# Expert gather with three row groups for U and three for V, V rows six groups behind, and the query block ahead of a chunk's weights

## The reference, cut to what matters

```python
q = (xblk @ w_query).reshape(B, TOKEN_BLOCK, N_PEER_HEADS, 2, SUBKEY_DIM)
s = jnp.einsum('bthpd,hpnd->bthpn', q, sub_keys)
vals, idx = lax.top_k(s, PEER_TOPK)
...
top_s, pos = lax.top_k(cand, PEER_TOPK)
eidx = jnp.take_along_axis(cand_idx, pos, axis=-1)
g = jax.nn.softmax(top_s, axis=-1)
h = jnp.einsum('btd,bthkd->bthk', xblk, expert_u[eidx])
act = jax.nn.gelu(h, approximate=False) * g
return jnp.einsum('bthk,bthkd->btd', act, expert_v[eidx])
```

## Time and profile before

| | us |
|---|---|
| median of 3 runs | 3295.08 |
| lowest and highest | 3289.69, 3298.97 |
| span of the profiled execution | 3263.7 |
| median less that span | 31.4 |
| expert gather, layer 0, first indirect DMA to last | 240.7 to 1010 |
| the same, layer 1 | 1230 to 1997 |

### The profile page before, as it was taken

The page is one execution under the profiler, slowest core; times in us unless marked ns, Lnnn a source line. Parts: engine busy times, 40 slices in busy tenths (PEclk is TensorE's granted clock), DMA queues, the critical chain, the costliest instruction groups (busy, mean ns, idle before and its releaser), DMA issues.

```text
span 3263.7 us, 34887 instructions
## 1 busy us (share of the span) xinstructions
PE 2431.9 (75%) x12607; PEld 1727.6 (53%) x12607; DVE 2088.5 (64%) x4416; ACT 933.8 (29%) x1486; POOL 1043.1 (32%) x1060
## 2 busy tenths in 40 slices
PE   5996555544546997555545545999999999999998
PEld 4754422221103764422221102789879988997797
DVE  7878576666656958576666654655555555556654
ACT  3511011110112421011101112544554446445543
POOL 0105566666663105566566663100010001000000
PEclk9998777766667998677666766989999999999999
DMA  9858999999999839999999998345534542554353
GB/s 363 299 209 332 353 374 380 378 379 365 361 378 341 295 139 342 350 370 394 377 359 372 356 365 307 131 143 191 180 130 155 180 168 82 190 194 155 110 193 123
DMA packets 308642, 886.31 MB, mean 272 GB/s; under 512 B 22824, under 2 KB 32144, under 8 KB 308240
## 3 DMA queue, kind: packets, MB, share of 16 engines
q0 software_dynamic: 147456, 536.94, 42.9%
q1 hardware_dynamic: 161040, 347.51, 29.9%
HBM read 883.32 MB, written 1.05 MB: 271 GB/s over the span
## 4 chain that ended last, share of the span: by engine, by line
PE 46%; issue 31%; DVE 9%; another core or an unknown queue 6%; DMA 4%; SPq 2%; ACT 2%; POOL 1%; DVEq 0%; ACTq 0%; POOLq 0%
PE lin L837 7%; PE lin L838 7%; PE lin L839 7%; PE psT L839 2%; PE psT L838 2%; PE psS L838 2%; PE psS L839 2%; PE psT L837 2%; PE psS L837 2%; PE lin L1141 2%; PE psS L1097 2%; PE psS L887 2%; DMA ring<-in_w_in 2%; PE lin L1014 1%
## 5 line engine op out<-in xcount | busy, mean ns | idle before, releaser
L2454 DVE CUSTOM_DVE_ANT_0 proj<-proj,psT 128x1024 f32<-128x1024 f32 x512 | 606.1, 1218 | 211.1 <-DMA proj<-in_expert_u,eidx 120.5
L1928 DVE TENSOR_TENSOR weights_split<-ring,weights_split 128x1024 fp32r<-128x1024 f32 (+1 forms) x360 | 431.5, 1207 | 376.2 <-ACT weights_split L1712 373.6
L2787 POOL DMA_INDIRECT proj<-in_expert_u,eidx x512 | 481.5, 940 | 424.7 <-DVEq L2430 212.7
L1712 ACT ACTIVATE weights_split<-ring 128x1024 fp32r<-128x1024 f32 (+1 forms) x376 | 391.5, 1046 | 467.7 <-PE lin L839 291.6
L1141 PE MATMUL lin<-vbuf,rowb 128*32 128x512 f32 x1024 | 252.0, 879 | 266.8 <-issue 180.4
L2823 POOL TENSOR_TENSOR weights_split<-ring,weights_split 128x1024 fp32r<-128x1024 f32 x16 | 37.9, 2376 | 995.3 <-ACT weights_split L1712 995.3
L1141 PE MATMUL lin<-ring,rowb 128*32 128x512 f32 x896 | 208.8, 755 | 153.1 <-issue 107.1
L837 PE MATMUL lin<-weights_split,xT_high 128*128 128x512 f32 (+1 forms) x736 | 295.0, 401 | 19.6 <-issue 8.2
L839 PE MATMUL lin<-weights_split,xT_high 128*128 128x512 f32 (+1 forms) x736 | 288.1, 391 | 0.0
L2800 POOL DMA_INDIRECT ring<-in_expert_v,pT x224 | 211.0, 942 | 231.4 <-remote 86.8
L2800 POOL DMA_INDIRECT vbuf<-in_expert_v,pT x256 | 241.2, 942 | 115.5 <-issue 76.5
(11 more groups left out here) (336 smaller groups left out, 4943.9 us busy)
## 6 DMA issues: line engine op xcount, KB each, us to landing
ring<-in_mlp_w_up SPq DMA_DIRECT2D x32, 2048.0 KB, 8.1
ring<-in_mlp_w_down SPq DMA_DIRECT2D x32, 2048.0 KB, 7.9
ring<-in_w_in SPq DMA_DIRECT2D x14, 2048.0 KB, 14.1
ring<-in_w_query SPq DMA_DIRECT2D x14, 2048.0 KB
vbuf<-in_ada_w SPq DMA_DIRECT2D x12, 2048.0 KB, 12.9
ring<-in_diff_w_in SPq DMA_DIRECT2D x11, 2048.0 KB, 8.1
proj<-in_ada_w SPq DMA_DIRECT2D x24, 512.0 KB, 5.1
ring<-in_moba_w_in SPq DMA_DIRECT2D x6, 2048.0 KB, 8.0
```

The lines of the kernel that those rows point to most:

```text
L1712: act.activation(part(p, 0, kind, w), raw_piece(slot, p, kind, w), ACT.Copy).then_inc(hi_ready, 1)
L1928: dve.tensor_tensor(part(p, 1, kind, w), raw_piece(slot, p, kind, w), part(p, 0, kind, w).bitcast(F32), ALU.subtract).then_inc(lo_ready, 1)
L2454: dve.tensor_tensor_reduce(ubuf[:, n % GB, :], ubuf[:, n % GB, :], x_row, 1.0, 0.0, ALU.mult, ALU.add, hdot[:, cb, k:k + 1]).then_inc(h_re ...
L2787: pool.indirect_dma_start(out=ubuf[:, (16 * c + k) % GB, :], out_offset=None, in_=table["u"], in_offset=bass.IndirectOffsetOnAxis(ap=eidx[ ...
```

## The change

U gets a third group of buffers, in ring slot 3, which was a V set; V keeps three sets. `UQUAD` says which U group goes where: the first four alternate between the two old ones, then the three rotate. So U(i) waits, but for the first few, for the dots of U(i-3), and V(q) for the sum of V(q-3). The last V group goes to U buffers. V(q) is issued behind U(q+6) for chunks 5 to 12, behind U(q+2) in chunks 0 and 1, and with a lag of 3, 4 and 5 in chunks 2 to 4 and of 5, 4 and 3 in the last three (`LAGS`). `stationaries(c)` of chunks 3 to 13 moves behind dot 3 of chunk c+1 (`SPREAD_BEHIND`, `SPREAD_STEP`), ahead of the quarter of the search there. In asking chunks from 4 on, keys, both halves of the query and the scores all come ahead of `weights_by_pair(c)`. `indices_by_pair(c+2)` comes ahead of a chunk's sums instead of between them.

```diff
-VLAG = 2
+NVB = 3
+GROUPS = 4 * PH * NT
+UQUAD = [0, 1, 0, 1] + [(2, 0, 1)[i % 3] for i in range(GROUPS - 4)]
+UBEFORE = [max([j for j in range(i) if UQUAD[j] == UQUAD[i]], default=None) for i in range(GROUPS)]
+VBUF = [q % NVB for q in range(GROUPS - 1)] + [NVB]
...
+SPREAD_BEHIND = range(3, NCH - 2)
+SPREAD_STEP = 3
+LAGS = [2, 2, 3, 4, 5] + [6] * (NCH - 8) + [5, 4, 3]
...
                 for c in range(1, NCH):
+                    if c in ASKED and c > 2:
+                        query_keys(ASKED[c])
+                        for part in range(4):
+                            query_rows(ASKED[c], part)
+                        key_scores(ASKED[c])
                     weights_by_pair(c)
-                    if c in ASKED and c > 1:
-                        query_keys(ASKED[c])
                     expert_sum(c)
...
                 for c in range(3, NCH):
-                    dots(c)
-                    stationaries(c)
+                    after = {4 * step + 3: [lambda step=step: topk_part(c + 2, step)] for step in range(4)} if c + 2 < NCH else {}
+                    if c - 1 in SPREAD_BEHIND:
+                        after[SPREAD_STEP] = [lambda: stationaries(c - 1)] + after.get(SPREAD_STEP, [])
+                    dots(c, after)
+                    if c not in SPREAD_BEHIND:
+                        stationaries(c)
...
-                    if n >= GB:
-                        pool.wait_ge(h_ready, n - GB + 4)
+                    if UBEFORE[i] is not None:
+                        pool.wait_ge(h_ready, 4 * UBEFORE[i] + 4)
...
-                        if 4 * c + g >= VLAG:
-                            v_rows(4 * c + g - VLAG)
+                        while q < NSET * NCH and q + LAGS[q // NSET] <= 4 * c + g:
+                            v_rows(q)
+                            q += 1
```

## The result

The changed kernel takes **3575.31 us** (median of 5 runs, 3571.02 to 3591.33) where the kernel before took 3298.97 in the same rounds: ratio **1.084**, 95% interval 1.082 to 1.087. I had predicted 3371 and a range up to 3465. Slower was right, the size wasn't: 276 us are lost and not 76.

The account below looks back on a forecast made before the run. Taken as bound: nearly full DMA plus POOL's pauses before V rows. Span 3263.7 plus 75.6 us for asking chunks gave 3339.3, with 31.4 around it 3371 us predicted; range 3240 to 3465.

Parts of the forecast that it names:

- What bounds the kernel: U(16) to U(60): DMA needs 41.2 us a chunk, chunks take 46.5; the gap is POOL's pauses before V rows, 78 us.
- The chain without lateness: From issue of U(4c+4) to issue of U(4c+8), through PE's sum and DVE's dots: 37.3 us plain, 58.6 us asking.
- The block of 21.3 us: Query block of asking chunks, between the sum of V(4c-1) and the weights: transposes, two halves, ACT's copies, scores.
- the excess: Asking chunks 6, 8 and 10: 63 us instead of 50.4, so 12.6 us each, 75.6 us in two layers.
- both bounds: Upper times of a chunk with reports late in full: 54.2 us plain, 72 us asking.
- I keep what plain chunks take now: Plain chunks stay at 45.7 us; the old pauses go and return as pauses before U rows.
- rival 1: Reports are late in full: plain chunks up to 54.2, asking ones 72 us; 3544 us in full, chance 0.17.
- The rest: Moved indices, first four chunks (up to 10 us gain a layer) and the end (up to 9 us loss): set at zero.
- nearly hidden: Query block in chunk 4: chunk 3's rows have lag 4 and land before chunk 4's dots end, so it costs little.
- The quarter of the search: DVE's search part on the chain, behind the stationaries and before four dots: 3.5 us taken.
- The 31.4 us around the span: Time added to the forecast span of 3339.3 us to give 3370.7 us.
- Rivals 2 and 3: 2: removed pauses pay for the query block, 3293 us, chance 0.13; 3: DVE's wait is covered, 3223 us, chance 0.24.

Follow-up runs that it names:

- Pacing: Three memsets of 0.33 us on POOL ahead of each group of four row issues, against the changed kernel otherwise unaltered: 3416 us, 1.041 of the kernel before.

## Why the prediction failed

**What bounds the kernel.** Right for the chip of the earlier trace rows: the pauses before V rows went (78 us to 24), and new ones came before U rows, with dots as releaser, as written. The rule that I had set aside, a core's share of about 358 GB/s (the Trainium skill, DMA: Bandwidth & Descriptors, Specifications), isn't what binds: 408 GB/s over 476 us.

**The chain without lateness: right.** It gave 37.3 us for plain chunks, under POOL's 39.8: measured 39.8 on the prompt chip. That is less than the 41.2 us of DMA that I had called a bound from below; over several chunks it still holds (374 GB/s in this stretch), since the DMA catches up in the pauses of the asking chunks. The chain gave 58.6 for asking ones: measured 829.0 - 770.5 = 58.5, and 57.9; the third is 64.0, behind a chunk of 35.3. The block of 21.3 us took 820.71 - 801.24 = 19.5.

**Luck in the excess.** The 37.8 us a layer that I forecast from U(16) to U(60) look right on the prompt chip, 512.1 - 476.2 = 35.9, but by two errors that cancel: the three asking chunks cost 180.4 - 124.8 = 55.6 us more, since they took 41 to 42 and not 50.4 before, and the other eight took 19.7 less.

**The step that failed: how much of the lateness falls on the chain.** The prediction had both bounds, 54.2 and 72 us. It kept 45.7 for plain chunks ("I keep what plain chunks take now") and took 4.4 of 14 us in asking ones. Measured were 53.6 to 54.4 and 72.9 to 74.0, the upper bounds, and up to 2 us over. The 45.7 was misread too: the nine "plain" chunks behind it have an asking one among them (chunk 8, 52.5 us from U(36) to U(40)). And it was the nearest row in value and not in kind: it is what a wait of POOL's for PE costs, one report that POOL's own pause sets free. The new wait goes from PE to DVE to POOL, and its first report falls due while POOL still has 10 us of rows to issue, so it has to wait for POOL to stop and the queue to run dry; each time. Against rival 1 I had said that an earlier pause of POOL's empties the queue earlier. There is no earlier pause, since the change took those away. Pacing shows it by its other end: with POOL at 357 GB/s chunks of the same kernel take 47.1 and 58.8 us. From U(16) to U(60) the loss was 634.1 - 512.0 = 122.1 us a layer, 37.8 of it forecast.

**"The rest" at zero.** In layer 0 the first row to U(16) takes 229.2 us instead of 203.6, and U(60) to the last row 72.2 instead of 53.9: 25.6 + 18.3 = 43.9 us a layer, and 28.0 + 20.2 on the prompt chip, by POOL's issues (9 us of the 20.2 come back there: from the last row of layer 0 to the first of layer 1 it takes 218.4 us instead of 227.8). One price behind it was wrong by its own step, "moving `indices_by_pair` ahead of the sums costs nothing". In chunk 1 PE waits there for DVE's indices, with all four sums behind it, and POOL waits for the first of those. PE and POOL of after, then PE of the kernel before on the prompt chip, where the first sum is at 337.50 and the indices (L1118) come behind two sums:

```profile
404.34 0.58 PE L1131 MATMUL psS<-const,pT 128*128 128x16 f32 x2 [22.25 <-DVE pT L2453]
```
```profile
408.79 0.94 POOL L2828 DMA_INDIRECT ring<-in_expert_v,pT  x1 [36.21 <-PE lin L1155]
```
```profile
337.50 1.92 PE L1141 MATMUL lin<-vbuf,rowb 128*32 128x512 f32 x16 [0.78 <-DVE rowb L2479]
...
365.72 0.29 PE L1118 MATMUL psS<-const,pT 128*128 128x16 f32 x2
```

That the wait exists is read from the trace; what it costs alone wasn't tried, and how much of it is the missing fourth V set stays open: every kernel above that has three V sets has both. Chunk 4, taken as "nearly hidden", has a pause of its own of 16.1 us (14.5 on the prompt chip).

**The sum.** 2 x (122.1 + 43.9) = 332 us, where the span grew by 3589.4 - 3263.7 = 326. By layer 84.3 us beyond the forecast are the step that failed, and 43.9 "the rest". The quarter of the search, taken at 3.5 us, took 939.37 to 941.21, 1.8: too little to matter.

**The 31.4 us around the span** were misread. In the later runs a time is 2 us above the span of the same execution (3139.6 and 3137.7). The profiled execution of the kernel before was a quick one, and there was nothing to add.

**The chances.** Rival 1 in full gave 3544 us; it had 0.17, and my range ended 79 us below it. Half of its 249 us would be 3420; the 3450 written there is about half of the way from the forecast to 3544. Its sign was written down (2.8 us steps that end when the queue is empty), and so was its price. Rivals 2 and 3 are dead: the query block ahead of the weights costs 117 us on its own on a late chip, and the changed kernel is slower on the prompt chip too.

## What to carry to other kernels

When a change moves a wait onto a chain through more engines, price each report on that chain at the worst lateness that the trace shows, unless a row shows it prompt under the same load; an average over old waits is no row for a new one. Look in the first iterations for waits that the steady state doesn't have before an edit of an engine's order is put at nothing. And compare kernels on one chip: 4.6 to 5.3% lay between chips here, as much as the change itself cost on the quicker one.

## What the runs showed of the hardware

- **Reports between engines can be late by 14 us and more** while row DMAs fill the core's DMA (407 to 409 GB/s), on three of the four chips that I can tell apart by the kernel before, which took 3282 to 3304 us there. The changed kernel shows 14.6 us from PE's start to ACT's. With the query block between the sums it is 23.5 once, 1617.60 to 1641.14, at 411 GB/s; there POOL issues again when ACT starts, and the rate is down to 360. On the fourth chip (3138 to 3141 us) ACT came within 1.2 us at the same rate and with a longer queue. What differs between the chips stays open: no run changed it.
- Late reports aren't the whole of it. The matmuls that creep at 2.8 us in the earlier trace rows stand inside one sum, where the kernel waits for nothing; they end with the full queue as well, but why an engine slows there stays open.
- **Issuing more slowly can be faster.** On late chips 357 GB/s of issue gave 3416 us where POOL at its own pace gave 3575, and 0.991 of the kernel before; 405 GB/s gave nothing. On the prompt chip pacing only cost (1.010 with two memsets, 1.066 against 1.050 with two, 1.063 against 1.023 with three).
- The same program keeps PE busy 253 us on a late chip and 199 on the prompt one, in the same eleven chunks at about the same clock (0.68 and 0.69).
